# Where the tiles of a long fp32 kernel stand within 128-byte lines, and which half of a line the weights' tiles take

## The reference

```python
for layer in range(DEPTH):
    x = x + mixer(x, *mixer_params[layer])
    x = x + peer_ffn(x, *ffn_params[layer])
...
x = x + 0.5 * m[2] * swiglu(modulate(x, norm_g[l, 0], m[0], m[1]), ffn1_wi[l], ffn1_wo[l])
h = modulate(x, norm_g[l, 1], m[3], m[4])
x = x + m[5] * y
x = x + 0.5 * m[8] * swiglu(modulate(x, norm_g[l, 2], m[6], m[7]), ffn2_wi[l], ffn2_wo[l])
```

## Time and profile before

| | |
|---|---|
| median of 3 executions | 3586.74 us |
| the three | 3586.74, 3586.43, 3600.17 us |
| the profiled execution | 3591.39 us |
| its span, first to last instruction | 3589.7 us |
| PE busy | 3211.6 us, 89% of the span |
| DVE, ACT, POOL busy | 2124.1, 1669.6, 673.7 us |
| mean granted TensorE clock | 0.946 |
| read from HBM | 562.29 MB, mean 158 GB/s |

### The profile page before, as it was taken

How to read it: one execution, slowest core, us unless ns; L and a number is a source line. 1 busy time by engine, 2 the same in 40 slices (tenths; PEclk the granted TensorE clock), 3 DMA queues, 4 the chain that set the end, 5 groups by cost and what they waited for, 6 DMA issues and landing times. The chain is left out here.

```text
span 3589.7 us, 67058 instructions
## 1 busy us (share of the span) xinstructions
PE 3211.6 (89%) x25390; PEld 3071.8 (86%) x25390; DVE 2124.1 (59%) x3228; ACT 1669.6 (47%) x2714; POOL 673.7 (19%) x515
## 2 busy tenths in 40 slices
PE   8689899879999679899869999999987889899798
PEld 7378899869998569899859998999976679899697
DVE  4746958887665565936796665333253655454654
ACT  4034576665554354576565554322134344354342
POOL 0315930003332014940003332000000010000000
PEclk9779999999999789999999999999998789899898
DMA  5135478317776135578417786222232135454353
GB/s 164 39 107 198 163 253 286 111 66 261 257 257 196 55 108 199 168 236 288 148 47 253 257 259 201 81 89 90 92 115 58 36 100 193 136 192 164 112 187 117
DMA packets 180618, 568.94 MB, mean 158 GB/s; under 512 B 22672, under 2 KB 31632, under 8 KB 179360
## 3 DMA queue, kind: packets, MB, share of 16 engines
q1 hardware_dynamic: 180512, 567.60, 48.0%
HBM read 562.29 MB, written 5.24 MB: 158 GB/s over the span
## 5 line engine op out<-in xcount | busy, mean ns | idle before, releaser
L209 DVE TENSOR_TENSOR peer_e_lo<-peer_raw,peer_e_hi 128x1024 fp32r<-128x1024 f32 x392 | 488.8, 1247 | 428.5 <-ACT peer_e_hi L205 428.4
L205 ACT ACTIVATE peer_e_hi<-peer_raw 128x1024 fp32r<-128x1024 f32 x512 | 539.3, 1054 | 287.8 <-PE peer_e_s L1112 183.2
L209 DVE TENSOR_TENSOR ffn_lo<-ffn_raw,ffn_hi 128x1024 fp32r<-128x1024 f32 x260 | 318.5, 1226 | 524.2 <-ACT ffn_hi L205 524.2
L205 ACT ACTIVATE ffn_hi<-ffn_raw 128x1024 fp32r<-128x1024 f32 x264 | 279.4, 1060 | 572.0 <-PE ffn_acc L1929 355.7
L1157 PE MATMUL peer_e_o<-x_normed,peer_e_hi 128*128 128x256 f32 x2048 | 479.5, 277 | 6.9 <-POOL x_normed L209 6.9
L1159 PE MATMUL peer_e_o<-x_normed,peer_e_hi 128*128 128x256 f32 x2048 | 479.2, 277 | 0.0
L209 POOL TENSOR_TENSOR x_normed<-peer_e_h,x_normed 128x256 fp32r<-128x256 f32 x256 | 217.8, 851 | 1078.5 <-ACT x_normed L205 1078.5
L1157 PEld LDWEIGHTS peer_e_o<-x_normed,peer_e_hi 128*128 128x128 f32 x2048 | 386.2, 189 | 7.2 <-issue 7.2
L1159 PEld LDWEIGHTS peer_e_o<-x_normed,peer_e_hi 128*128 128x128 f32 x2048 | 386.4, 189 | 0.0
L1920 PE MATMUL ffn_acc<-x_normed,ffn_hi 128*128 128x256 f32 x1408 | 358.4, 285 | 21.8 <-DVE x_normed L295 19.5
L1921 PE MATMUL ffn_acc<-x_normed,ffn_hi 128*128 128x256 f32 x1408 | 354.1, 282 | 0.0
(11 more groups left out here) (564 smaller groups left out, 7580.9 us busy)
## 6 DMA issues: line engine op xcount, KB each, us to landing
peer_raw<-in_l_down SPq DMA_DIRECT2D x256, 512.0 KB, 4.2
peer_raw<-in_l_up SPq DMA_DIRECT2D x256, 512.0 KB, 4.5
ffn_raw<-in_ffn_wi SPq DMA_DIRECT2D x176, 512.0 KB, 3.5
peer_e_wm<-in_w_mod SPq DMA_DIRECT2D x144, 512.0 KB, 5.1
ffn_raw<-in_ffn_wo SPq DMA_DIRECT2D x88, 512.0 KB, 3.3
l_in_raw<-in_l_w_in SPq DMA_DIRECT2D x39, 512.0 KB, 3.9
peer_q_raw<-in_l_peer_w_query SPq DMA_DIRECT2D x32, 512.0 KB, 4.0
wg_in_raw<-in_w_in SPq DMA_DIRECT2D x26, 512.0 KB, 3.9
```

What stands on the lines that cost most here:

```text
L205: return act.activation(hi, v, ACT.Copy)
L209: return eng.tensor_tensor(lo, v, hi.bitcast(F32), ALU.subtract)
```

## The change

The tiles are padded to 128 bytes in place of 64, some small tiles are joined in one, and each pair `hi`, `lo` of weights gets 64 bytes of padding ahead and behind. So every tile made through the helper begins at half 0, and every `hi` and `lo` of weights at half 1. Instructions, their order, their waits and all sizes stay as they are.

```diff
-def tile_at_64(nc, stack, name, shape, dt=F32):
+LINE = 128
+
+def tile_in_lines(nc, stack, name, shape, dt=F32):
     tile = stack.enter_context(nc.sbuf_tensor(name, shape, dt))
-    if -(-math.prod(shape[1:]) * 4 // 32) % 2:
-        stack.enter_context(nc.sbuf_tensor(f"{name}_pad", [P, 8], F32))
+    over = -(-math.prod(shape[1:]) * 4 // 32) * 32 % LINE
+    if over:
+        stack.enter_context(nc.sbuf_tensor(f"{name}_pad", [P, (LINE - over) // 4], F32))
     return tile
+
+def weight_tiles(nc, stack, name, shape):
+    stack.enter_context(nc.sbuf_tensor(f"{name}_before", [P, LINE // 8], F32))
+    hi = stack.enter_context(nc.sbuf_tensor(f"{name}_hi", shape, F32R))
+    lo = stack.enter_context(nc.sbuf_tensor(f"{name}_lo", shape, F32R))
+    stack.enter_context(nc.sbuf_tensor(f"{name}_after", [P, LINE // 8], F32))
+    return hi, lo
...
-    K.eps = sb("eps", [P, 1])
-    K.lb = sb("lower_bound", [P, AH])
-    K.nlb = sb("one_less_lower_bound", [P, AH])
+    small = sb("eps_and_lower_bounds", [P, 1 + 2 * AH])
+    K.eps, K.lb, K.nlb = small[:, 0:1], small[:, 1:1 + AH], small[:, 1 + AH:]
...
-        hi = st.sb("hi", [P, pairs, UNIT], F32R)
-        lo = st.sb("lo", [P, pairs, UNIT], F32R)
+        hi, lo = weight_tiles(nc, st.ctx, name, [P, pairs, UNIT])
...
-        hi = st.sb("hi", [P, 2, D], F32R)
-        lo = st.sb("lo", [P, 2, D], F32R)
+        hi, lo = weight_tiles(nc, st.ctx, st.name, [P, 2, D])
...
-        den = st.sb("den", [P, TT * PH])
-        rden = st.sb("rden", [P, TT * PH])
+        dens = st.sb("dens", [P, 2, TT * PH])
+        den, rden = dens[:, 0], dens[:, 1]
...
-        hi, lo = st.sb("hi", [P, 2, D], F32R), st.sb("lo", [P, 2, D], F32R)
+        hi, lo = weight_tiles(nc, st.ctx, name, [P, 2, D])
```

More of the change, by code:

```diff
@@ L89, in sb @@
     def sb(self, name, shape, dt=F32):
-        return tile_at_64(self.nc, self.ctx, f"{self.name}_{name}", shape, dt)
+        return tile_in_lines(self.nc, self.ctx, f"{self.name}_{name}", shape, dt)
     def ps(self, name, shape):
@@ L128, in sb @@
     def sb(name, shape, dt=F32):
-        return tile_at_64(nc, keep, name, shape, dt)
+        return tile_in_lines(nc, keep, name, shape, dt)
     K.x = sb("x_stream", [P, DC, T])
@@ L1298, in _ @@
             tops = choice[:, 2].rearrange("p (a j) -> p a j", j=PK)
-            chain(dve.tensor_copy(den[:].unsqueeze(2), tops[:, :, 0:1]))
-            dve.tensor_tensor(tops, tops, den[:].unsqueeze(2).to_broadcast([P, TT * PH, PK]), ALU.subtract)\
+            chain(dve.tensor_copy(den.unsqueeze(2), tops[:, :, 0:1]))
+            dve.tensor_tensor(tops, tops, den.unsqueeze(2).to_broadcast([P, TT * PH, PK]), ALU.subtract)\
                 .then_inc(shifted, 1)
@@ L1337, in _ @@
                     dve.wait_ge(exped, 1)
-                    chain(dve.tensor_reduce(den[:], tops, AX_X, ALU.add))
-                    chain(dve.reciprocal(rden[:], den[:]))
-                    dve.tensor_tensor(tops, tops, rden[:].unsqueeze(2).to_broadcast([P, TT * PH, PK]), ALU.mult)\
+                    chain(dve.tensor_reduce(den, tops, AX_X, ALU.add))
+                    chain(dve.reciprocal(rden, den))
+                    dve.tensor_tensor(tops, tops, rden.unsqueeze(2).to_broadcast([P, TT * PH, PK]), ALU.mult)\
                         .then_inc(chosen, 1)
@@ L1703, in sb @@
         def sb(name, shape, dt=F32):
-            return tile_at_64(nc, keep, f"mla_{name}", shape, dt)
+            return tile_in_lines(nc, keep, f"mla_{name}", shape, dt)
         cq, ckv, kpe = sb("cq", [P, 2, T]), sb("ckv", [P, 1, T]), sb("kpe", [P, TT, ROPE])
@@ L2101, in sb @@
         def sb(name, shape, dt=F32):
-            return tile_at_64(nc, keep, f"wg_{name}", shape, dt)
+            return tile_in_lines(nc, keep, f"wg_{name}", shape, dt)
         mix = sb("mix", [P, DC, T])
@@ L2111, in eb @@
             def eb(name, shape, dt=F32):
-                return tile_at_64(nc, early, f"wg_{name}", shape, dt)
+                return tile_in_lines(nc, early, f"wg_{name}", shape, dt)
             q = eb("q", [P, TT, 512])
```

## The result

| | before | after |
|---|---|---|
| median, executions in one comparison | 3599.83 us, 6 | 3630.23 us, 6 |
| lowest and highest | 3586.43, 3603.96 us | 3625.06, 3645.39 us |
| ratio after / before, 95% interval | | 1.0099, 1.0071 to 1.0127 |
| the profiled execution | 3591.39 us | 3627.41 us |
| its span | 3589.7 us | 3625.7 us |

The forecast was 3552 us. The kernel came out 78 us above it, on the other side of the kernel before. The sum said 34.5 us faster; measured side by side it was 30.4 us slower.

A forecast was written before the change was run, and what follows sets the result against it. PE's matmul steps times their number, plus seams between stages, were taken to bound the kernel. Savings of 17.1 + 11.6 + 2.9 + 4.9 - 2.0 = 34.5 us off the median 3586.7 gave 3552 us, range 3543 to 3575.

The forecast's parts named there:

- Items 1 to 4: SwiGLU second phases, ffn1_0's first phase, l_in's form "f", l_out with wg projections: shorter steps save 17.1, 11.6, 2.9, 4.9 us.
- Item 5: Form "t" matmuls with 512 columns in l0_in, l1_in and wg_in: slower in different halves, 2.0 us lost.
- Item 6: peer_q, peer_e, first phases of ffn2_0, ffn1_1, ffn2_1, context's blocks: 16,224 matmuls already in different halves, unchanged.
- Items 7 to 9: Cuts on DVE, ACT, POOL, loads into raw tiles, and what is late next: all 0, no new stall.
- The draw: Streams in different halves sometimes start at 0.1177 and keep it: a ninth of 16,224 matmuls, 0.0044 us each.
- the longer step becomes the rule: Rival: starts in different halves mostly take the longer step; 14,400 matmuls lose 64 us, time 3646; chance 0.03.
- the newly parted matmuls fall into 0.1177: Rival: matmuls newly put in different halves reach only 0.1177, saving 9 us, time 3577; chance 0.06.
- No change at all, 3587: Rival: the half is not the cause but something that goes with the stage, so nothing moves; chance 0.04.
- The base: Median of the kernel before, 3586.7 us, 4.7 below the profiled execution, from which the saving was subtracted.

The follow-up runs named there:

- the bursts: Separate kernels without the model: TensorE repeats the expert stage's matmuls in bursts at chosen operand distances; 0.1133 us a step at 64, 0.1178 in nearly all at 192.

## Why the prediction was wrong

- **Items 1 to 4, the steps of operands in the same half.** That 0.1200 belongs to tiles in one half, and that moving them apart is worth something, held: with all pairs at 64 the second phases and ffn1_0 come to 0.1133. But the change puts them at 192, where 0.1178 is the usual step (in ffn1_0's first phase it puts x at 192 and the context at 64, which comes to 0.1176), so together they won some 12 us of the 36.5 put down, and only ffn2_0's second phase drew 0.1133.
- **Item 5, 512 columns slower: right**, 411 ns for 404, and 0.2334 for 0.2267 in the bursts.
- **Item 6 is the step that failed.** "Unchanged, since they are in different halves already": the halves stayed, but the distance went from 64 to 192 modulo 256, and 16,224 matmuls moved from a place where some seven long stretches in ten run at 0.1133 to one where nine in ten run at 0.1178. Counted at 0 in the sum; it cost about 54 us in the profiled execution, more than all that the other items won. The witnesses I had for "different halves" all had the stationary tile 64 bytes ahead (in the context's blocks of wg_in the activations are the stationary ones), so the rows could not tell "another half" from "64 bytes ahead". The addresses would have raised the doubt, and the changed ones could be worked out without building anything.
- **Items 7 to 9: right.** Cuts 1227 and 2743 ns, no new wait, PE full in the stretches.
- **The mechanism behind the steps.** What I read as a collision for half a line when both operands stand in one half is not what the bursts show: 0 and 128 are both the same half and have 0.1200 and 0.1187, and 64 and 192 are both the other half and have 0.1133 and 0.1178. What happens between the two reads is not shown.
- **The draw.** Its existence, its two steps and its price (0.0044 a matmul) were right. Wrong was that it keeps its ninth: the odds go with the distance.
- **The rivals.** The slower one, "the longer step becomes the rule", is what happened, at the place and by the mechanism it named, 3646 against 3630 measured; it had a chance of 0.03, because "the peer_e and peer_q pairs keep the relation that gives 0.1133 now". That sentence took the half for the relation. The rival before it, that the newly parted matmuls fall into 0.1177, came true beside it, for all but ffn2_0's second phase. No change at all, 3587, is outside what was measured.
- **The base.** The median before, 3586.74 of three, was low: later medians of the same kernel were 3592.7 to 3599.8. That is up to 13 us of the miss, and the draw is the likely cause, which no run singles out.

With the distances at 64, what the forecast wanted is there: the profiled execution at 3550.29 us is within 2 us of the 3552, though the median is 3571, as a good quarter of the long stretches at 64 still draws the longer step (22 of 76).

## What to carry to other kernels

When a step is explained by where tiles stand, work out all the addresses, before and after, and look at what else the witnesses have in common; a padding that looks harmless can move every operand pair by 128 bytes. In streams of fp32r matmuls of 256 columns with a weight load each, put the stationary tile 64 bytes past a multiple of 256 from the moving one: here that was worth 0.6 to 0.8% over the kernel before and 1.7% over the opposite arrangement. Where 512 columns of weights move past stationary activations the best of the places tried is another, the same place modulo 256 (0.2267); the stationary tile 64 ahead, that is the weights 192 ahead, is the slowest (0.2334). A kernel whose executions spread by 1% may be drawing at each start of its streams, so compare several profiles by stretch before naming a cause. And read a step from one start to the next where a stretch is short: its edges can hold matmuls at the lower clock.

## What the runs showed of the hardware

- The start-to-start step of fp32r matmuls with 256 moving columns at 2.4 GHz depends on the stationary tile's distance ahead of the moving one modulo 256 bytes: 0.1133 us at 64, 0.1178 at 192 (3 of 24 bursts at 0.1133), 0.1200 at 0 and 160, 0.1183 at 32, 0.1187 at 128.
- It is not symmetric: 64 ahead and 64 behind (192) differ by 4%.
- At one distance there can be two steps, 0.1133 and 0.1178, each kept until the stream stops: 12 bursts to 4 at distance 64 and 0 to 16 at 192 after the clock's rise, 54 long stretches to 22 and 4 to 42 in the model.
- A stream with half its matmuls at 64 and half at 192 steps at 0.1176.
- 512 moving columns have an order of their own: with the moving weights 0, 64, 128, 192 ahead of the stationary tile 0.2267, 0.2289, 0.232, 0.2334.
- ScalarE and VectorE working on SBUF beside the stream changed none of this.
